# Prompt attention: output products taken one unit later, two unused 256-column products per unit, transposed weights in two buffers

## The reference

```python
s_c = einsum('bcgqd,bngd->bcgqn', q, kc) * scale + bias ; p_c = masked_softmax(s_c)
o_c = jnp.einsum('bcgqn,bngd->bcgqd', p_c.astype(vc.dtype), vc)
...
p_s = masked_softmax(s_s, (dist_s >= 0)[:, :, :, None, :])
o_s = jnp.einsum('bcgqk,bcgkd->bcgqd', p_s.astype(v_sel.dtype), v_sel)
...
p_w = masked_softmax(s_w, mask_w[None, :, None, None, :])
o_w = jnp.einsum('bcgqw,bwgd->bcgqd', p_w.astype(vw.dtype), vw)
g = jax.nn.sigmoid(gate.astype(jnp.float32))
o = g[..., 0:1] * o_c + g[..., 1:2] * o_s + g[..., 2:3] * o_w
```

## Time and profile before

| | us |
|---|---|
| median of 3 timed runs | 1892.09 (1890.37 to 1898.02) |
| the profiled execution, its own time | 1885.86 |
| its span, first to last instruction | 1884.0 |
| PE busy | 1756.9 (93%) |
| PE weight loads busy | 1675.9 (89%) |
| DVE busy | 836.2 (44%) |
| ACT busy | 525.2 (28%) |
| the block of the change | about 198 to 329 of the span |

### The profile page before, as it was taken

The page is one execution under the profiler, slowest core; times in us unless marked ns, Lnnn a source line. Parts: engine busy times, 40 slices in busy tenths (PEclk is TensorE's granted clock), DMA queues, the critical chain, the costliest instruction groups (busy, mean ns, idle before and its releaser), DMA issues. The chain is left out here.

```text
span 1884.0 us, 36115 instructions
## 1 busy us (share of the span) xinstructions
PE 1756.9 (93%) x15724; PEld 1675.9 (89%) x15724; DVE 836.2 (44%) x1654; ACT 525.2 (28%) x896; POOL 695.9 (37%) x278
## 2 busy tenths in 40 slices
PE   6999788779768998999999999999999999999997
PEld 5987677569745997899999999999999999999997
DVE  4251686226582444465530355444245555024431
ACT  5132455323331222232221222322123222112221
POOL 1200000013102111465553565655565665445541
PEclk8988799999878999899999999999999999999999
DMA  5540420522201000222223222322222222322222
GB/s 145 123 58 23 159 80 13 163 69 73 60 1 30 29 4 27 67 68 90 85 68 96 79 78 65 93 91 89 85 76 87 75 83 73 85 92 89 72 72 77
DMA packets 158379, 140.90 MB, mean 75 GB/s; under 512 B 16178, under 2 KB 153942, under 8 KB 157838
## 3 DMA queue, kind: packets, MB, share of 16 engines
q1 hardware_dynamic: 158222, 138.60, 24.9%
HBM read 132.68 MB, written 10.02 MB: 76 GB/s over the span
## 5 line engine op out<-in xcount | busy, mean ns | idle before, releaser
L270 POOL TENSOR_TENSOR w_lo<-w_raw,w_hi 128x2048 fp32r<-128x2048 f32 (+3 forms) x109 | 459.3, 4214 | 776.4 <-ACT w_hi L264 776.3
L309 PE MATMUL ps<-h_hi,w_hi 128*128 128x288 f32 x2016 | 434.2, 296 | 0.0
L309 PE MATMUL ps<-h_lo,w_hi 128*128 128x288 f32 x2016 | 433.0, 296 | 0.0
L309 PE MATMUL ps<-h_hi,w_lo 128*128 128x288 f32 x2016 | 432.9, 296 | 0.0
L264 ACT ACTIVATE w_hi<-w_raw 128x2048 fp32r<-128x2048 f32 (+3 forms) x109 | 190.0, 1743 | 503.2 <-PE ps L309 458.5
L309 PEld LDWEIGHTS ps<-h_hi,w_hi 128*128 128x128 f32 x2016 | 324.0, 189 | 0.3
L309 PEld LDWEIGHTS ps<-h_lo,w_hi 128*128 128x128 f32 x2016 | 323.8, 189 | 0.0
L309 PEld LDWEIGHTS ps<-h_hi,w_lo 128*128 128x128 f32 x2016 | 323.5, 189 | 0.0
L418 DVE TENSOR_TENSOR xT<-ps,xT 128x576 f32<-128x576 f32 x48 | 35.6, 756 | 264.7 <-PE ps L309 264.7
L309 PE MATMUL ps<-g_hi,w_hi 128*128 128x288 f32 x704 | 151.0, 295 | 0.0
L309 PE MATMUL ps<-g_hi,w_lo 128*128 128x288 f32 x704 | 150.9, 295 | 0.0
(11 more groups left out here) (499 smaller groups left out, 2767.6 us busy)
## 6 DMA issues: line engine op xcount, KB each, us to landing
w_raw<-in_ffn_up SPq DMA_DIRECT2D x44, 1024.0 KB, 5.1
w_raw<-in_ffn_down SPq DMA_DIRECT2D x16, 768.0 KB, 4.8
w_raw<-in_w_in_odd SPq DMA_DIRECT2D x12, 1024.0 KB, 5.1
w_raw<-in_ffn_down SPq DMA_DIRECT2D x16, 640.0 KB, 4.4
w_raw<-in_w_in_even SPq DMA_DIRECT2D x7, 1024.0 KB, 5.5
w_raw<-in_w_in_even SPq DMA_DIRECT2D x6, 872.0 KB, 10.3
BT<-rv SPq DMA_DIRECT2D x8, 520.0 KB, 3.6
seg<-in_cache_cmp_kv SPq DMA_DIRECT2D x32, 128.0 KB
```

What stands on the lines that cost most here:

```text
L270: pool.tensor_tensor(slab_view(wlo[slot], st), slab_view(raw[slot], st), slab_view(whi[slot], st).bitcast(F32), ALU.subtract).then_inc(w_l ...
L309: last = pe.matmul(ps[:, bank + 2 * j + half, 0:HT], w[slot][:, c:c + 128], x[:, xs + t, half * HT:(half + 1) * HT], start=(t == 0 and n = ...
```

## The change

PE now runs transposes(u), outputs(u-1), scores(u+2) in iteration u, with outputs(31) behind the loop. At the head of each outputs stand FILL = 2 products of 256 columns, queries times keys, into columns 256 to 511 of bank 7, which nothing reads. They wait for o_taken, but stand ahead of the waits for the copies. PTs, PTw and PTc exist twice, den has four slots. The copies of u wait for o_ready of u-2, exps(u) waits for o_taken of u-4. On DVE the weighted sum of u-1 stands between den(u) and masked_max(u+2); before, the weighted sum of u stood behind masked_max(u+2).

```diff
-            PTs = r.take("PTs", [128, 4, 128])
+            PTs = [r.take("PTs", [128, 4, 128]) for _ in range(2)]
...
-            den = r.take("den", [128, 2, 3])
+            den = r.take("den", [128, 4, 3])
...
+            FILL = 2
...
+                    def outputs(u):
+                        h, qt, s = u // 4, u % 4, u % 2
+                        g = h // 4
+                        if u >= 1:
+                            pe.wait_ge(o_taken, u)
+                        for _ in range(FILL):
+                            pe.matmul(ps[:, 7, 256:512], q_st[g][:, u // 4 % 4, 128 * qt:128 * qt + 128], k_mv[0][0][g][:, 0:256], start=True, stop=True)
+                        pe.wait_ge(pt_act, u + 1)
+                        pe.wait_ge(pt_dve, u + 1)
+                        O = ps[:, 7, 0:192]
...
+                        last.then_inc(o_ready, 1)
...
                         pe.transpose(ps[0:32, 4, 256:384], sC[s][:, :], ident[:, :]).then_inc(pt_ready, 1)
+                        if u >= 1:
+                            outputs(u - 1)
                         if u + 2 < U:
                             scores(u + 2)
-                        pe.wait_ge(pt_act, u + 1)
-                        pe.wait_ge(pt_dve, u + 1)
-                        if u >= 1:
-                            pe.wait_ge(o_taken, u)
...
+                    outputs(U - 1)
...
                         dve.wait_ge(pt_ready, u + 1)
+                        if u >= 2:
+                            dve.wait_ge(o_ready, u - 1)
...
                         if u >= 1:
+                            weighted(u - 1)
                         if u + 2 < U:
                             masked_max(u + 2)
-                        dve.wait_ge(o_ready, u + 1)
...
+                    weighted(U - 1)
...
-                        if u >= 2:
-                            act.wait_ge(o_taken, u - 1)
+                        if u >= 4:
+                            act.wait_ge(o_taken, u - 3)
```

More of the change, by code:

```diff
@@ L1510, in even_mixer @@
             sC = [r.take("s_cmp", [128, 32]) for _ in range(2)]
-            PTs = r.take("PTs", [128, 4, 128])
-            PTw = r.take("PTw", [128, 4, 128])
-            PTc = r.take("PTc", [32, 128])
+            PTs = [r.take("PTs", [128, 4, 128]) for _ in range(2)]
+            PTw = [r.take("PTw", [128, 4, 128]) for _ in range(2)]
+            PTc = [r.take("PTc", [32, 128]) for _ in range(2)]
             mx = r.take("mx", [128, 2, 3])
-            den = r.take("den", [128, 2, 3])
+            den = r.take("den", [128, 4, 3])
             bt_in, s_ready, s_taken, p_ready, pt_ready, pt_act, pt_dve, o_ready, o_taken, m_ready = (sem(x) for x in (
@@ L1574, in scores @@
                         last.then_inc(s_ready, 1)
+                    def outputs(u):
[8 more added lines that the diff above has]
+                        O = ps[:, 7, 0:192]
+                        pe.matmul(O[:, 0:64], PTc[s][:, :], vc[0:32, 2, 64 * g:64 * g + 64], start=True, stop=True)
+                        for n, (PT, c0) in enumerate(((PTs[s], 896), (PTw[s], 1152))):
+                            for kt in range(qt + 1):
+                                last = pe.matmul(O[:, 64 * (n + 1):64 * (n + 2)], PT[:, kt, :], zq[:, kt, c0 + 64 * g:c0 + 64 * g + 64],
+                                                 start=(kt == 0), stop=(kt == qt))
+                        last.then_inc(o_ready, 1)
                     scores(0)
@@ L1578, in _ @@
                         h, qt, s = u // 4, u % 4, u % 2
-                        g = h // 4
                         pe.wait_ge(p_ready, u + 1)
@@ L1627, in masked_max, with weighted @@
                         dve.tensor_scalar(mx[:, s, :], mx[:, s, :], -1.0, None, ALU.mult).then_inc(m_ready, 1)
+                    def weighted(u):
+                        h, qt, s = u // 4, u % 4, u % 2
+                        dve.wait_ge(o_ready, u + 1)
+                        O, out = ps[:, 7, 0:192], onat[:, qt, 64 * h:64 * h + 64]
+                        dve_chain(dve, dve.tensor_scalar(out, O[:, 0:64], den[:, u % 4, 0:1], None, ALU.mult))
+                        dve_chain(dve, dve.scalar_tensor_tensor(out, O[:, 64:128], den[:, u % 4, 1:2], out, ALU.mult, ALU.add))
+                        dve.scalar_tensor_tensor(out, O[:, 128:192], den[:, u % 4, 2:3], out, ALU.mult, ALU.add).then_inc(o_taken, 1)
                     masked_max(0)
@@ L1632, in _ @@
                         dve.wait_ge(pt_ready, u + 1)
-                        if u >= 1:
[L1634 to L1640, removed]
+                        if u >= 2:
+                            dve.wait_ge(o_ready, u - 1)
+                        dve.tensor_copy(PTw[s][:, 0:qt + 1, :], ps[:, 6, 0:128 * (qt + 1)].rearrange("p (a b) -> p a b", b=128)).then_inc(pt_dve, 1)
+                        dve.wait_ge(p_ready, u + 1)
+                        dve_chain(dve, dve.tensor_scalar(den[:, u % 4, :], den[:, u % 4, :], 1e-30, None, ALU.max))
+                        dve_chain(dve, dve.reciprocal(den[:, u % 4, :], den[:, u % 4, :]))
+                        dve_chain(dve, dve.tensor_tensor(den[:, u % 4, :], den[:, u % 4, :], gpr[:, qt, 3 * h:3 * h + 3], ALU.mult))
+                        if u >= 1:
+                            weighted(u - 1)
                         if u + 2 < U:
                             masked_max(u + 2)
-                        dve.wait_ge(o_ready, u + 1)
[L1644 to L1647, removed]
+                    weighted(U - 1)
                 @block.scalar
@@ L1654, in exps @@
                         act.wait_ge(m_ready, u + 1)
-                        if u >= 2:
-                            act.wait_ge(o_taken, u - 1)
-                        act.activation(sC[s][:, :], sC[s][:, :], ACT.Exp, bias=mx[:, s, 0:1], accum_out=den[:, s, 0:1])
-                        act.activation(sS[s][:, 0:nk], sS[s][:, 0:nk], ACT.Exp, bias=mx[:, s, 1:2], accum_out=den[:, s, 1:2])
-                        act.activation(sW[s][:, 0:nk], sW[s][:, 0:nk], ACT.Exp, bias=mx[:, s, 2:3], accum_out=den[:, s, 2:3]).then_inc(p_ready, 1)
+                        if u >= 4:
+                            act.wait_ge(o_taken, u - 3)
+                        d = u % 4
+                        act.activation(sC[s][:, :], sC[s][:, :], ACT.Exp, bias=mx[:, s, 0:1], accum_out=den[:, d, 0:1])
+                        act.activation(sS[s][:, 0:nk], sS[s][:, 0:nk], ACT.Exp, bias=mx[:, s, 1:2], accum_out=den[:, d, 1:2])
+                        act.activation(sW[s][:, 0:nk], sW[s][:, 0:nk], ACT.Exp, bias=mx[:, s, 2:3], accum_out=den[:, d, 2:3]).then_inc(p_ready, 1)
                     exps(0)
                     for u in range(U):
-                        qt = u % 4
+                        qt, s = u % 4, u % 2
                         act.wait_ge(pt_ready, u + 1)
[L1664 to L1667, removed]
+                        if u >= 2:
+                            act.wait_ge(o_ready, u - 1)
+                        act.copy(PTc[s][:, :], ps[0:32, 4, 256:384]).then_inc(ptc_act, 1)
+                        act.copy(PTs[s][:, 0:qt + 1, :], ps[:, 5, 0:128 * (qt + 1)].rearrange("p (a b) -> p a b", b=128)).then_inc(pt_act, 1)
                         if u + 1 < U:
```

## The result

The changed kernel takes 1946.22 us in the median of four runs (1930.23 to 1951.82), the kernel before on the same chip 1891.39: a ratio of 1.0262, with a 95% interval of 1.0225 to 1.0299; the quotient of the medians, 1.029, lies inside it. In the medians it is slower by 55 us, not by the 21 of the forecast. The direction was right, the size was not, and the time lies 21 us above 1925, the upper end of the range. The profiled execution is the slowest of the four, 1951.82 us with a span of 1950.0. Its four runs spread over 22 us, the four of before over 8.

A forecast was written before the change was run, and what follows sets the result against it. The prediction took a ring through DVE, with PE's outputs, as the new bound: +18.8 for 27 periods, +1.9 end, +0.6 head, together +21.3, so 1907.2 us against the profiled execution, 1913.4 as median; range 1903 to 1925.

The forecast's parts named there:

- The ring: Through DVE, from one Tc (a unit's last transpose) to the next: 16.63 us a group of four units against 13.84.
- the end: From the last Tc to the end of the last weighted sum: 6.5 us against 4.65, +1.9.
- the head: Units 0 to 3 at 1.2 GHz: Tc(4) at 225.5, +0.6, with bounds of -4 and +4.
- The relief: PE no longer waits for same-unit copies, nor ACT for the previous unit's weighted sum; by itself this shortens two rings.
- PE's own work in a group: Outputs 6.68, scores 2.7 and transposes 3.4 for four units, taken as about 12.4 us, below 13.84.
- rival C: Weighted sum not on the ring, PE's 12.4 us a group the bound: -9.8, 1882 us; chance 0.05.
- The clock: Expected to stay full; the rival, a drop inside the block, cost +20 to +25, about 1935 us, chance 0.10.
- should hold it: The two products add 512 columns to each unit, beside scores of 576 to 2112, and should hold the full clock.
- The price: At 1.2 GHz a group takes over 6.5 us longer: outputs some 5.4, plus Tc and the products.
- The rule that the prediction cited: Skill text: transposes do not count as busy like other products; avoid long idle gaps between bursts. Makes a clock drop likelier.
- D: Products raise the clock early, hand-overs overlap: -4 in the head, -6 over 28 units; +11, 1903 us; chance 0.12.

## Why the prediction was wrong

**The ring, right.** DVE's new order, the wait for the outputs ahead of the masked maxima and the wait of Tc behind them are all in the waits of the changed kernel. With the clock held the group was 16.98 us against the forecast 16.63. Part of the difference has a place: the outputs began 0.17 us after the end of Tc where the prediction took 0.06 (249.23 against 249.06 in the changed kernel). Two products cost about 0.17 a unit, not nothing; without them the group was 16.28. That the total with the clock held, before + 22 us, is so near the forecast + 21.3 is in part luck. In the profiled execution the 27 periods were 21.2 longer where the sum had 18.8, the end 2.7 where it had 1.9, and the head gave back 4.1 where the sum had a loss of 0.6; that gain came with the six products that the change does not have.

**The relief, right but worth nothing.** PE's wait for the copies went, as said, and so did ACT's for the weighted sum; both rings were shorter than the one through DVE, so nothing of it reached the time. PE's own work in a group was added up wrongly: 6.68, 2.7 and 3.4 make 12.8, not 12.4, and the runs with scores first and no products, where PE binds, measured 13.03. It bore only on rival C.

**The clock, wrong.** The step that failed is the sentence that the two products "should hold it". The prediction gave the fall of the clock a chance of 0.10 and, if half of the groups ran so, 1935 us. The fall came, and it was larger: a mean of 0.64 over 144 us. The two products did not hold the clock: it was 0.62 from 222 to 320 with them and 0.61 without, and it was held only with six in the wait or eight at the head. The rows spoke for the fall: the clock had gone down within 321 to 322 while PE ran small outputs behind a wait of 1.09 us. The argument against it was the 98 us at 1.00, but those belong to a group of 13.84 us, and a group of 15.2 in the same order already loses the clock at times.

Why two are too few is not shown. Counting columns of scores and unused products over a group does not explain it: the kernel before has 5376 in 13.84 us, 388 a us, and held the clock; the changed one has 7424, which is 437 a us in the 16.98 us measured with the clock held, and lost it. What the later runs show is on which side each kernel falls: periods of 15.2 a group in PE's old order lose the clock part of the time, and so do two products ahead of Tc in the new one, while six there hold it at a group of 16.3, and eight at the head of the outputs at 19.7.

The price was low too: 25.7 us for a group at 1.2 GHz, measured, is 9 above the full clock, and I had 6.5. I had stretched the outputs, Tc and the products, and left out that PE's scores and transposes then no longer fit beside DVE's work: from 295 to 321, at 0.50, PE is busy 24.69 of 26 us, and the Tc of units 18 and 19 wait for nothing on DVE.

The Trainium skill (TensorE: Matmul & The Clock Gate, A second HAM failure mode: psum-queue depth-cycling) describes a kernel in which PE idles briefly but often between groups of products, and the clock goes up and down with it. The trace agrees in so far as the clock went up and down while no wait of PE from 236 on was longer than 1.1 us. It does not agree that such waits decide alone: with eight products at the head of the outputs PE waited 1.12, 0.94 and 0.81 us in the same places and the clock stayed at 1.00. The rule that the prediction cited, on long idle gaps, was not the one that bore on this change.

**The other rivals.** C, the faster side, did not come: the weighted sum is on the ring, as the run with only DVE's order swapped shows from the other side. D, an early full clock, came the other way round: it rose at 236 in place of 222. With six more products in the wait, or with eight at the head, D's early rise did come, 2.5 and 3.9 us behind the first Tc.

**What stays open.** How the clock is decided was not measured, only on which side of it each kernel falls. Why the full clock comes 14 us later in the changed kernel's head is not explained. In the kernels with scores ahead of outputs, with products or without, it came within 4 us of the first Tc. Why the first Tc of the block starts anywhere between 204 and 219 us in different profiles was not tried. Nor was a second bank for the outputs, which would take the weighted sum off the ring.

## What to carry to other kernels

Before moving work between engines that hand it round a ring, write down the ring for the new order, with every wait of an in-order engine as a link; a delay of one unit only helps if the wait that it adds is not on that ring. A longer period can cost twice where TensorE is not full: once for itself and once if the clock falls. Here the second part was about as large as the first by the ratios, and larger by the medians, 33 of 55 us. A clock that held at one period is no evidence that it holds at a longer one, and some unused products are no evidence either; run the kernel with and without them. In these runs unused products paid only inside a wait that existed anyway, and in sufficient number, and even then they only undid part of the loss: 1913 us against 1890 before the change.

## What was not expected of the hardware

- A few products decide between 1.2 and 2.4 GHz in this loop: two in the wait of three units in four gave a mean clock of 0.72 and 1936 us, six gave 1.00 and 1915 us.
- More PE work made the kernel faster: with 144 products more than the changed kernel it took 33 us less in the medians.
